# Fourth layer's attention: two heads per block in row and column halves, mask on TensorE

## The reference

```
s_lat = jnp.where(valid, s_lat, -jnp.inf)
s_ctx = jnp.einsum("bqhgd,bchd->bhgqc", qb, ck) * scale
m = max(max(s_lat), max(s_ctx), sink_g)
den = sum(exp(s_lat - m)) + sum(exp(s_ctx - m)) + exp(sink_g - m)
o = (exp(s_lat - m) @ v_lat + exp(s_ctx - m) @ v_ctx) / den
y = o @ w_out
```

## Time and profile before

| | |
|---|---|
| median of 3 runs | 2397.06 us (2397.05 to 2399.03) |
| the profiled execution | 2399.51 us, span 2397.4 us |
| PE busy | 2251.4 us, 94% of the span |
| PEld | 1877.1 us, 78% |
| DVE | 1677.5 us, 70% |
| ACT | 885.1 us, 37% |
| POOL | 674.4 us, 28% |
| chain of work that ended last | PE 79%, DVE 13%, issue, POOL and ACT 2% each, DMA 1% |
| mean granted clock | 0.975 |

### The profile page before, as it was taken

The page is one execution under the profiler, slowest core; times in us unless marked ns, Lnnn a source line. Parts: engine busy times, 40 slices in busy tenths (PEclk is TensorE's granted clock), DMA queues, the critical chain, the costliest instruction groups (busy, mean ns, idle before and its releaser), DMA issues.

```text
span 2397.4 us, 31162 instructions
## 1 busy us (share of the span) xinstructions
PE 2251.4 (94%) x12408; PEld 1877.1 (78%) x12408; DVE 1677.5 (70%) x2431; ACT 885.1 (37%) x1357; POOL 674.4 (28%) x434
## 2 busy tenths in 40 slices
PE   5999999899999979999989799988999998899998
PEld 5887778688888768888988577766888887558997
DVE  6765566997777974767778776779777775596443
ACT  0313333232233232444443446733223334243444
POOL 3001110223344510203365113323334461002244
PEclk9999999999999989999999899999999999799999
DMA  8422124445555453345755442134555554204552
GB/s 275 150 78 86 62 72 170 145 162 189 184 185 194 154 176 97 100 155 165 240 172 171 134 148 67 66 96 153 191 194 175 193 158 116 53 1 123 177 180 84
DMA packets 268024, 341.14 MB, mean 142 GB/s; under 512 B 31056, under 2 KB 181464, under 8 KB 267624
## 3 DMA queue, kind: packets, MB, share of 16 engines
q1 hardware_dynamic: 266704, 334.92, 43.5%
q10 hardware_dynamic: 1176, 4.23, 0.5%
HBM read 338.04 MB, written 1.08 MB: 141 GB/s over the span
## 4 chain that ended last, share of the span: by engine, by line
PE 79%; DVE 13%; issue 2%; POOL 2%; ACT 2%; DMA 1%; SPq 0%; POOLq 0%; ACTq 0%; DVEq 0%
PE PS L648 23%; PE PS L649 22%; PE PS L650 22%; DVE bias L1571 4%; DVE w_l L1542 2%; PE PS L889 2%; PE PS L912 2%; PE PS L716 1%; DVE work L1716 1%; DVE a_l L1730 1%; PE PS L1065 1%; PE PS L899 1%; PE PS L1091 1%; PE PS L844 1%; POOL a_l L2120 1%
## 5 line engine op out<-in xcount | busy, mean ns | idle before, releaser
L648 PE MATMUL PS<-a_h,w_h 128*128 128x512 f32 (+1 forms) x2808 | 974.4, 347 | 43.4 <-DVE a_l L1730 28.3
L649 PE MATMUL PS<-a_l,w_h 128*128 128x512 f32 (+1 forms) x2808 | 960.6, 342 | 0.0
L650 PE MATMUL PS<-a_h,w_l 128*128 128x512 f32 (+1 forms) x2808 | 960.2, 342 | 0.0
L1542 DVE TENSOR_TENSOR w_l<-ring,w_h 128x1024 fp32r<-128x1024 f32 (+1 forms) x420 | 578.4, 1418 | 229.9 <-ACT w_h L1172 229.3
L648 PEld LDWEIGHTS PS<-a_h,w_h 128*128 128x128 f32 x2808 | 539.4, 192 | 142.0 <-issue 60.3
L1172 ACT ACTIVATE w_h<-ring 128x1024 fp32r<-128x1024 f32 (+1 forms) x420 | 412.8, 1032 | 572.3 <-PE PS L650 518.8
L650 PEld LDWEIGHTS PS<-a_h,w_l 128*128 128x128 f32 x2808 | 539.7, 192 | 59.6
L649 PEld LDWEIGHTS PS<-a_l,w_h 128*128 128x128 f32 x2808 | 540.0, 192 | 55.6
L1571 DVE SCALAR_TENSOR_TENSOR bias<-ring,silu,bias 128x512 f32<-128x512 f32 x532 | 453.8, 908 | 4.2 <-DMA ring<-in_w_mod 0.5
L2120 POOL TENSOR_TENSOR a_l<-hid,a_h 128x2048 fp32r<-128x2048 f32 (+1 forms) x60 | 228.2, 3804 | 241.6 <-ACT a_h L1196 241.6
L2135 POOL TENSOR_TENSOR hid<-hid 128x256 f32<-128x256 f32 (+1 forms) x128 | 161.2, 1261 | 411.7 <-ACT hid L1154 411.7
(11 more groups left out here) (183 smaller groups left out, 2385.7 us busy)
## 6 DMA issues: line engine op xcount, KB each, us to landing
ring<-in_w_ff SPq DMA_DIRECT2D x64, 1024.0 KB, 5.6
ring<-in_ffn_w SPq DMA_DIRECT2D x64, 1024.0 KB, 5.5
ring<-in_w_mod SPq DMA_DIRECT2D x48, 1024.0 KB, 5.2
ring<-in_ada_w SPq DMA_DIRECT2D x48, 1024.0 KB, 5.2
ring<-in_w_in SPq DMA_DIRECT2D x42, 1024.0 KB, 5.3
ring<-in_mlstm_w_in SPq DMA_DIRECT2D x12, 1024.0 KB, 5.7
ring<-in_w_o SPq DMA_DIRECT2D x8, 1024.0 KB, 5.1
ring<-in_w_attn_out SPq DMA_DIRECT2D x4, 1024.0 KB, 5.8
```

Source lines behind the costliest of these rows:

```text
L648: nc.tensor.matmul(out, stat[0], mov[0], start=start, stop=False, **kw)
L649: nc.tensor.matmul(out, stat[0], mov[1], start=False, stop=False, **kw)
L650: return nc.tensor.matmul(out, stat[1], mov[0], start=False, stop=stop, **kw)
L1542: V.tensor_tensor(w_l[:, n % 2, c], ring[:, split_raw[n] % SLOTS, c], w_h[:, n % 2, c].bitcast(F32), ALU.subtract).then_inc(s_wl, 1)
```

## The change

`rope` and `attn` of this layer go, and a phase `s_heads` comes. `s_in` now takes keys first (as the tile that follows the norm, 512 columns wide), then values, then two tiles of queries, with rotations 8, 9 (keys) after the values and 0 to 3 (queries) after the second query tile. The other two query tiles, each of two units and two rotations, are worked inside `s_heads`, one unit or rotation in each of the first eight blocks, all in bank 0.

`s_heads` runs over 16 blocks. A block is two heads (they lie in the lower and upper 64 partitions of `sq_` and `sk`) and 128 of the 256 queries. Scores of the two heads are two products on 64 rows each; the mask is added by two more matmuls, the identity times the rounded mask (`ident_r`, `mask_r`, made once by VectorE, which `s_masked` reports). Three sets of two banks (1 to 6) hold scores, and the transposed probabilities are written over them. VectorE takes the maximum of both heads, with the sinks negated beforehand, and scales the probabilities of both (new wait on `s_rinv` between the inverse and the scaling). ScalarE takes the exponentials and copies all transposed probabilities of a block in one instruction of 128x1024. The values of a pair of blocks are eight products of 64 columns, alternating between the column halves, in bank 7. VectorE writes the outputs of two heads together, 128x256. Three of the weight tiles' roundings and splits lie inside the phase.

The diff, cut (the old loops that go are in the kernel above):

```diff
-            phase("s_in", tiles=(2,) * 5 + (4,), **base)
-            phase("rope", units=10, chunks=10, **base)
-            heads = [("lat", h) for h in range(16)]
-            phase("attn", heads=heads, **base)
-            n["head"] += len(heads)
+            turns = lambda *cs: tuple(("rope", c) for c in cs)
+            phase("s_in", tiles=(2, 4, 2, 2), extra={1: turns(8, 9), 3: turns(0, 1, 2, 3)}, **base)
+            phase("s_heads", tiles=(2, 2), extra={0: turns(4, 5), 1: turns(6, 7)}, banks=(0,), **base)
+            n["head"] += 8
             phase("to_h", tiles=(2,) * 4, src="attn", gate=2, name="s_out", **base)
...
+        mask_r = x0_l[:, 3, :].rearrange("p (q n) -> p q n", q=2)
+        ident_r = x0_l[:, 2, LAT:LAT + P]
...
+        probsT = (work[:, 4:6, :].rearrange("p a (k n) -> p a k n", k=4),
+                  big[:, 12:16, :].rearrange("p (a b) n -> p a (b n)", a=2).rearrange("p a (k n) -> p a k n", k=4))
...
-                    whole(w, 1024 + 256 * i)
+                    whole(io["swa_w_in_2"][0], 1024 + 256 * i)
+                for t in range(2):
+                    query_tile(t)
+            elif kind == "s_heads":
+                for t in range(2, 4):
+                    query_tile(t)
...
+        def set_banks(u):
+            return slice(1 + 2 * (u % 3), 3 + 2 * (u % 3))
+        def probs(u):
+            return work[:, u % 3, :].rearrange("p (a n) -> p a n", a=2)
...
+            def turned_unit(ph, c):
+                if ph["block"] == 0:
+                    return ph["steps"][3 + c // 2]["u"] + c % 2
+                s_in = plan[plan.index(ph) - 1] if ph["kind"] == "s_heads" else ph
+                if c >= 8:
+                    return s_in["steps"][0]["u"] + c % 2
+                return (s_in["steps"][2 + c // 2] if c < 4 else ph["steps"][c // 2 - 2])["u"] + c % 2
...
-                    first_tile(ph["steps"][0], ph["x"] - KC)
+                    first_tile(ph["steps"][0], ph["x"] - KC, width=ALL)
                     for i, st in enumerate(ph["steps"][1:], 1):
                         w, u = tile(st), st["u"]
                         for j in range(st["units"]):
-                            if i == 5:
+                            if i == 1:
                                 tokm(st, u + j, w, j)
                             else:
-                                fm(st, u + j, w, slice(P * j, P * j + P), from_a, ALL if i == 4 else LAT)
-                        mod_unit(st)
+                                fm(st, u + j, w, slice(P * j, P * j + P), from_a, LAT)
+                        if i == 1:
+                            pe.wait_ge(s_aux, AUX_LANDED[3])
+                        for e, (what, j) in enumerate(st["extra"]):
+                            small_unit(ph, u + st["units"] + e, what, j)
+                elif kind == "s_heads":
+                    x0, p0 = ph["head"], ph["head"]
+                    def pair_scores(v):
+                        ch, qt = v // 2, v % 2
+                        if v >= 3:
+                            pe.wait_ge(s_pta, x0 + v - 2)
+                        S = PS[:, set_banks(v), :]
+                        for a in range(2):
+                            nc.tensor.matmul(S[:, a, :], sq_[HD * a:HD * a + HD, ch, P * qt:P * qt + P],
+                                             sk[HD * a:HD * a + HD, ch // 4, :], start=True, stop=False,
+                                             skip_group_check=True)
+                        for a in range(2):
+                            mm = nc.tensor.matmul(S[:, a, 0:LAT], ident_r, mask_r[:, qt, :], start=False, stop=True,
+                                                  skip_group_check=True)
+                        mm.then_inc(s_sc, 1)
+                    def pair_turn(v):
+                        pe.wait_ge(s_probd, v + 1)
+                        for a in range(2):
+                            for k in range(4):
+                                mm = nc.tensor.transpose(PS[:, 1 + 2 * (v % 3) + a, P * k:P * k + P],
+                                                         probs(v)[:, a, P * k:P * k + P], ident[:, :])
+                        mm.then_inc(s_tr, 1)
+                    def pair_values(p):
+                        pe.wait_ge(s_pta, x0 + 2 * p + 2)
+                        if p:
+                            pe.wait_ge(s_o, p0 + p)
+                        for k in range(4):
+                            for a in range(2):
+                                kv = 2 * (p // 4) + a
+                                mm = nc.tensor.matmul(PS[HD * a:HD * a + HD, 7, 0:LAT], sv[:, k, HD * kv:HD * kv + HD],
+                                                      probsT[p % 2][:, a, k, :], start=(k == 0), stop=(k == 3),
+                                                      skip_group_check=True)
+                        mm.then_inc(s_pv, 1)
+                    def dense(v):
+                        if v >= 8:
+                            return
+                        st = ph["steps"][v // 4]
+                        j = v % 4
+                        if j < 2:
+                            fm(st, st["u"] + j, tile(st), slice(P * j, P * j + P), from_a, LAT)
+                        else:
+                            small_unit(ph, st["u"] + j, *st["extra"][j - 2])
+                    wait_units(pe, u)
+                    pe.wait_ge(s_masked, 1)
+                    pair_scores(0)
+                    pair_scores(1)
+                    for v in range(16):
+                        dense(v)
+                        if v % 2 == 0 and v:
+                            pair_values(v // 2 - 1)
+                        if v + 2 < 16:
+                            if (v + 2) % 4 == 0 and v + 2 >= 8:
+                                wait_unit(pe, ph["steps"][(v + 2) // 4 - 2]["u"] + 3)
+                            pair_scores(v + 2)
+                        pair_turn(v)
+                    pair_values(7)
...
+                    def pair_exps(v):
+                        act.wait_ge(s_nm, x0 + v + 1)
+                        if v >= 3:
+                            act.wait_ge(s_tr, x0 + v - 2)
+                        for a in range(2):
+                            nc.scalar.activation(probs(v)[:, a, :], PS[:, 1 + 2 * (v % 3) + a, :], ACT.Exp,
+                                                 bias=nmax[:, v % 4, a:a + 1], accum_out=rsum[:, v % 4, a:a + 1])
+                        nc.scalar.activation(esink[:, v % 4, :], esink[:, v % 4, :], ACT.Exp).then_inc(s_exp, 1)
+                    def pair_turned(v):
+                        p, qt = v // 2, v % 2
+                        act.wait_ge(s_tr, x0 + v + 1)
+                        if p >= 2:
+                            act.wait_ge(s_pv, p0 + p - 1)
+                        nc.scalar.activation(probsT[p % 2][:, :, :, P * qt:P * qt + P],
+                                             PS[:, set_banks(v), :].rearrange("p a (k n) -> p a k n", k=4), ACT.Copy
+                                             ).then_inc(s_pta, 1)
+                    round_w(ph["s"] + 1)
+                    pair_exps(0)
+                    for v in range(16):
+                        if v:
+                            pair_turned(v - 1)
+                        if v + 1 < 16:
+                            pair_exps(v + 1)
+                        if v < 8 and v % 4 < 2:
+                            st = ph["steps"][v // 4]
+                            copy_unit(st["u"] + v % 4, sq_[:, 4 + 2 * (v // 4) + v % 4, :], slice(0, LAT), scale=QSCALE)
+                        if v in (2, 6):
+                            round_w(ph["s"] + 2 + v // 4)
+                    pair_turned(15)
...
+                        if i == 0:
+                            dve.wait_ge(s_aux, AUX_LANDED[3])
+                            V.tensor_scalar(nsink[:, :], sink[:, :], -1.0, None, ALU.mult)
+                            V.tensor_copy(ident_r, ident[:, :])
+                            V.tensor_copy(mask_r, aux[:, A_MASK:A_MASK + 512].rearrange("p (q n) -> p q n", q=2)
+                                          ).then_inc(s_masked, 1)
+                        for e, (what, c) in enumerate(st["extra"]):
+                            small_unit(ph, u + st["units"] + e, what, c)
...
+                    def pair_max(v):
+                        m = nmax[:, v % 4, :]
+                        dve.wait_ge(s_sc, x0 + v + 1)
+                        step(V.tensor_reduce(m, PS[:, set_banks(v), :], AX_X, ALU.max))
+                        step(V.scalar_tensor_tensor(out=m, in0=m, scalar=-1.0, in1=pair_sinks(nsink, v),
+                                                    op0=ALU.mult, op1=ALU.min))
+                        V.tensor_tensor(esink[:, v % 4, :], m, pair_sinks(sink, v), ALU.add).then_inc(s_nm, 1)
+                    def pair_inverse(v):
+                        r = rsum[:, v % 4, :]
+                        dve.wait_ge(s_exp, x0 + v + 1)
```

(70 more changed lines are left out.)

184 lines of the change are left out of this document (19 added, 165 removed).

## The result

The changed kernel takes 2384.85 us in the median of 4 runs (2382.88 to 2389.64), the kernel before 2398.05 beside it: a ratio of 0.9946 [0.993, 0.9963], 13.2 us faster. The forecast was 2390.6. The profiled execution took 2382.88 (span 2381.1), 16.6 less than that of before.

A forecast was written before the change was run, and what follows sets the result against it. PE and VectorE were both taken as full in the attention. First scores at 2052.4 plus 107.3 of attention end at 2159.7 against 2166.19, 6.5 us gained: 2390.6, range 2378 to 2402.

The forecast's parts named there:

- R1: Rival, attention blocks: clock survives the short stalls (2384.6; no low clock 2378.5) or scores overlap wholly (6.7 saved); chance 0.28.
- Projection: Before attention: keys multiplied under the norm, two query tiles moved, four rotations bare; first scores at 2052.4, before 2074.55.
- Scores: Attention blocks: four 64-row score instructions half overlapped, 1.28 us; 1.62 a block with mask and change.
- R2: Rival, scores in the attention blocks: row halves don't overlap, 7.0 us more, 2397.6, no change; chance 0.18.
- Mode changes: Attention blocks: a change between half and whole array costs 0.10, added once to the scores and once to the values.
- R3: Rival: each change of array mode waits until the array is empty, 0.16 at 40 changes, 4.2 more, 2394.8; chance 0.06.
- Copy: Attention blocks: PE waits for ScalarE's copy, one instruction of 1.08 us, 1.32 a block with latency and hand-overs; 13.6 in all.
- Bank 0: First eight blocks: PE idles 3.5 us three times for a rotation queued on VectorE to leave bank 0; 10.5 in all.
- Clock: Attention: half clock adds 6.1 us at the first scores and 2.0 behind each of three stalls, +6.0.
- R4: Rival, slower: the clock stays low in blocks 8 to 15, doubling 27.2 us of PE work, 2418; chance 0.07.
- R5: Rival: the column halves of the values don't overlap here, 14 us more, 2405; chance 0.06.

The follow-up runs named there:

- the serial run: Changed kernel with the values' loops exchanged, all products of one column half, then all of the other: 2392.29 us, 0.9961 of the kernel before.

## Why the prediction was right, and where it was off

The direction, the place and the kinds of waits came as forecast. The gain is 13.2 where I had 6.5; the time is 5.7 below the forecast, inside the range and at R1's 2384.6. That it falls on R1's figure is luck: of R1's two ways only the overlap of the scores came true, worth 3.6 with the changes of shape taken off, where R1 had 6.7, and other terms, above all the copy, made up the rest.

**Projection: right.** The first scores were put at 2052.4 with the norm where it was; they came 48.7 after the norm's matmul, which from 2003.16 is 2051.9. The wide key tile at half clock had its matmuls 0.427 apart (forecast 0.43), and the clock rose at about 2012.8, earlier than the 2016 I took from the earlier trace rows. The first tile then ended 19.2 after the norm's matmul; the four bare rotations ran from 2044.70 to 2050.35, 5.65 as in the sum. Of the 22.7 gained, 11.5 is the two query tiles that moved into the blocks, 3.5 the order of the tiles (the run with keys first), and the rest, 7.7, I put down to six of ten rotations that are no longer bare, 6 x 1.25 = 7.5.

**Scores: right kind, wrong size.** I chose 1.28, half overlapped, between 0.86 and 1.72. The runs show the lowest end, 0.86 (four instructions in 1.06, two in 1.05), and 0.20 for the changes of array around them instead of 0.10. The group cost 1.39 to 1.40 and not 1.62: -3.6. My reason for the middle was the column halves at 0.106 an instruction, which I read as an overlap for column halves only; it already was the whole overlap, half of the 0.223 of one half alone, and I should have carried that ratio over. R2 fell with it. The Trainium skill's page TensorE: Matmul & The Clock Gate, Part 3, was right that row tiles run side by side.

**Mode changes: R3's mechanism is there, its price bought back.** The changes cost 0.20 in the two slots of the scores, about 0.1 in the first slot of the mask (0.33 for two of 0.12) and 0.16 in the first and the last slot of the values (1.88 for 16 instructions of 0.107). A change thus shows on both sides, in the last slot ahead of it and in the first behind it. My 0.10, read from the earlier trace rows, was only the first part: in the same trace L844's first slot behind L870 is 0.53 instead of 0.43. Over 40 changes 5.9 is 0.15 each, nearer to R3's 0.16 than to my 0.10. That is in accord with the Trainium skill's TensorEngine Tiling (Array Packing), Key Properties, that a change of mode drains the engine. In all they cost 16 x (0.20 + 0.09) + 8 x 0.16 = 5.9 where I had 24 x 0.10 = 2.4; the result doesn't show it because the overlap of the rows gave more, 16 x 0.42 = 6.7. (R3's 4.2 more is 4.0 by its own terms, 40 x 0.16 - 24 x 0.10.)

**Copy: mis-sized.** 1.02 us and a wait of 1.11 a block, not 1.08 and 1.32; 10.2 in all against 13.6: -3.4.

**Bank 0: right.** 3.24, 3.24 and 3.31 against 3.5 each, at L767 in blocks 3 and 7 and at the query unit in block 4, with the queue of VectorE that I had named ahead of the rotation. The run with the rotation ahead removes them all.

**Clock: right sum, wrong split.** I had 6.1 at the start and 2.0 behind each stall, 12.1. From the slots: the first two score groups took 2.72 and 1.75 instead of 1.40, 1.7 lost; rotation and scores behind the first stall 1.6; the query unit (5.39 for 2.88) and values behind the second 2.7; rotation, scores and transposes behind the third 2.6; the last values 3.46 for 1.95, 1.5, which I had not foreseen: three waits of 1.1 stood just ahead of them. Together 10.1. The step that failed is the start: I argued from the old heads, which stayed low for 20 us, but here the clock was back at about 2053.8, after 3.4 us, within the second score group and before the first query unit, most of which I had put at half clock: 1.7 lost, not 6.1. R1's first half, that the clock survives stalls of 3.3, is refuted: it fell at all three.

**Sum.** The blocks were forecast at 107.3 and took 100.3: -3.6 for the scores, -3.4 for the copy, -2.0 for the clock, -0.7 for bank 0, together -9.7, and 2.7 back. Of these 0.4 is the three query units at full clock, at 2.96, 3.04 and 3.05 instead of 2.88, and 0.6 the values at 1.88 instead of 1.81; the other 1.7 I haven't broken down.

**R4 and R5.** R5 fell: values at 0.107 and a change, and the serial run lost only 0.91 a pair. R4 didn't happen here, though it is no phantom: with the mask between the row halves the late blocks ran at half clock for 57 of 64 us.

What isn't settled: why that run stays low for 30 us and the changed kernel for 6.8 behind the same wait, both with the same waits of 1.1 us. The runs give the cases, not the reason. And no run takes the query tiles back out of the blocks, so what their place there is worth by itself isn't measured.

## What to carry to other kernels

When heavy units are threaded into a fine-grained pipeline, look at what the evacuation of their bank is queued behind: here one moved helper call was worth 17 us, more than the whole change, because each wait of 3.3 us cost another 1.6 to 2.7 in low clock. Put a consumer one block later than the producer of its buffer where the buffers allow it. Alternate products on opposite halves, rows or columns, and put operations on the whole array behind both, since each change of shape cost 0.1 to 0.2 us here and the overlap was lost with it.

## What the hardware showed that I had not expected

- Products of 64 rows in the two row halves overlap wholly in float32: four instructions of 512 columns in 1.06 us with the changes of shape around them, against 1.05 for two of one half, and starts in pairs 0.007 us apart.
- With one column half's products behind the other's, four of each still run side by side where the halves meet: 2.79 us for 16 instructions, between 1.88 (alternating) and 3.6 (none).
- Filling PE until the first scores did not hold the clock: one idle of 2.75 us behind them brought 13.7 us at half clock.
- The clock fell with no wait above 1.2 us just ahead of it, in the blocks with serial row halves (2163) and ahead of the last values of the changed kernel (about 2146).
